# Third layer's q, k, v and gated input projections in three fp32r terms

## What is computed

```
hn = rms_norm_2(h, ln_mix[i])
z  = hn @ a_w_in[j]                       # 1024 x 3072
q, k, v, b_gate, c_gate, hc = split(z)    # six parts of 512
q, k = rope_partial(q), rope_partial(k)
attn = diff_attention(q, k, v, lam, lambda_init, a_subln[j])     # 4 heads, two maps each
conv = b_gate * causal_short_conv(c_gate * hc, a_conv_w[j])
h = h + concat([attn, conv]) @ a_w_out[j]
```

## Time and profile before

| | us |
|---|---|
| median of 3 runs | 1997.77 (1997.6 to 1998.2) |
| the profiled execution | 1994.57 |
| its span, first to last instruction | 1992.8 |
| PE busy in the span | 1924.8 (97%) |
| DVE busy | 1452.1 (73%) |
| ACT busy | 1013.4 (51%) |

### The profile page before, as it was taken

How to read it: one execution, slowest core, us unless ns; L and a number is a source line. 1 busy time by engine, 2 the same in 40 slices (tenths; PEclk the granted TensorE clock), 3 DMA queues, 4 the chain that set the end, 5 groups by cost and what they waited for, 6 DMA issues and landing times.

```text
span 1992.8 us, 30177 instructions
## 1 busy us (share of the span) xinstructions
PE 1924.8 (97%) x12687; PEld 1755.4 (88%) x12687; DVE 1452.1 (73%) x1742; ACT 1013.4 (51%) x1156; POOL 76.9 (4%) x122
## 2 busy tenths in 40 slices
PE   6999999999999999999999999999999999999997
PEld 5878878788788868999999898989898989898986
DVE  7888995774765346665455588888888888888873
ACT  3512121535465213444345577666676677667754
POOL 4010000000000100100220000000000000000000
PEclk9999999999999999999999999999999999999998
DMA  9945221453522431456753389999999999999981
GB/s 345 310 127 190 70 65 67 146 188 110 206 90 86 171 119 61 158 177 193 208 207 108 145 308 345 361 332 353 349 363 331 349 352 360 333 352 353 353 301 38
DMA packets 225858, 452.31 MB, mean 227 GB/s; under 512 B 6944, under 2 KB 91176, under 8 KB 225720
## 3 DMA queue, kind: packets, MB, share of 16 engines
q1 hardware_dynamic: 222128, 444.39, 63.6%
q0 software_dynamic: 1904, 5.80, 1.0%
q10 hardware_dynamic: 1688, 0.15, 0.1%
HBM read 448.21 MB, written 2.10 MB: 226 GB/s over the span
## 4 chain that ended last, share of the span: by engine, by line
PE 86%; DVE 8%; ACT 3%; issue 1%; DMA 1%; SPq 0%; POOL 0%; ACTq 0%; DVEq 0%; POOLq 0%
PE bank L1224 25%; PE bank L1250 12%; PE bank L2645 8%; PE bank L973 6%; PE bank L2411 4%; PE bank L1008 3%; PE bank L1056 2%; PE bank L856 2%; PE bank L897 2%; PE bank L774 2%; PE bank L1332 2%; PE bank L2906 1%; PE bank L762 1%; PE bank L2380 1%; PE bank L1235 1%
## 5 line engine op out<-in xcount | busy, mean ns | idle before, releaser
L2143 DVE TENSOR_TENSOR ring_r<-ring,his_r 128x2816 fp32r<-128x2816 f32 (+1 forms) x192 | 586.6, 3086 | 39.0 <-ACT his_r L1647 38.6
L1647 ACT ACTIVATE his_r<-ring 128x2816 fp32r<-128x2816 f32 (+1 forms) x192 | 491.0, 2561 | 185.7 <-DMA ring<-in_moe_w_dram 179.4
L1224 PE MATMUL bank<-his_r,hg_r 128*128 128x352 f32 x2048 | 353.4, 324 | 0.0
L1224 PEld LDWEIGHTS bank<-his_r,hg_r 128*128 128x128 f32 x2048 | 332.0, 188 | 0.6
L2645 PE MATMUL bank<-hT,ring 128*128 128x256 f32 x912 | 207.1, 383 | 1.4 <-ACT hT L3008 0.9
L2645 PEld LDWEIGHTS bank<-hT,ring 128*128 128x128 f32 x912 | 169.9, 190 | 27.9 <-issue 5.3
L1224 PE MATMUL bank<-ring_r,hg_r 128*128 128x352 f32 x1024 | 186.2, 324 | 0.0
L1224 PEld LDWEIGHTS bank<-ring_r,hg_r 128*128 128x128 f32 x1024 | 169.2, 189 | 0.0
L3293 DVE SCALAR_TENSOR_TENSOR arena<-ring,cw,arena 128x256 f32<-128x256 f32 x240 | 96.5, 477 | 0.1
L1250 PE MATMUL bank<-his_r,at_hi_r 128*128 128x512 f32 x352 | 92.9, 397 | 0.0
L1250 PE MATMUL bank<-his_r,at_lo_r 128*128 128x512 f32 x352 | 92.5, 396 | 0.0
(11 more groups left out here) (584 smaller groups left out, 3043.7 us busy)
## 6 DMA issues: line engine op xcount, KB each, us to landing
ring<-in_moe_w_dram SPq DMA_DIRECT2D x128, 1408.0 KB, 8.4
ring<-in_moe_w_dram SPq DMA_DIRECT2D x48, 1536.0 KB, 8.7
ring<-in_even_w_in_dram SPq DMA_DIRECT2D x28, 1024.0 KB, 6.2
ring<-in_ffn_w_dram SPq DMA_DIRECT2D x22, 1024.0 KB, 5.3
ring<-in_ada_w_dram SPq DMA_DIRECT2D x20, 1024.0 KB, 10.8
ring<-in_odd_w_in_dram SPq DMA_DIRECT2D x9, 2048.0 KB, 7.9
ring<-in_moe_w_dram SPq DMA_DIRECT2D x16, 1024.0 KB, 6.5
ring<-in_a_w_in_dram SPq DMA_DIRECT2D x6, 2048.0 KB, 7.9
```

The costliest lines, as they stand in the source:

```text
L1224: ins = mm(bank[first + m][:, 0:WC], x[:, KT // 2 * late + k, :], w[:, k, WC * m:WC * m + WC], start=(not late and k == 0 and s == "hg_hi" ...
L1647: A(moe_hi(n), moe_w(n), ACT.Copy).then_inc(sem("moe_hi"), 1)
L2143: V.tensor_tensor(moe_lo(n), moe_w(n), moe_hi(n).bitcast(F32), ALU.subtract).then_inc(sem("moe_lo"), 1)
```

## The change

It writes the input of `qk`, `v` and `bch` as a high part `hx_r` (in the place of `hT`) and a low part `xl_r` (in old gate space), cuts the weights into 12 halves of 128x2048 (u = 0 to 3 `qk`, 4 and 5 `v`, 6 to 11 `bch`), casts each half on ACT (`d_cast`) and subtracts on DVE (`d_low`), and multiplies three terms. The order of `qk` tiles 4 to 7 in PSUM changes to banks 7, 0, 1, 2.

```diff
+        with nc.sbuf_tensor("hx_r", [P, KT, T], F32R) as hx_r:    # over hT
+        xl_r = sb_r("xl_r", 7176, KT, T)
+        D_HI = [dw_r[off][:, :, :] for off in (19456, 11776, 21504, 25088, 27376, 19456, 11776, 25088, 27376, 25088, 27376, 25088)]
+        D_FREE = {5: ("qk", 2), 6: ("qk", 4), 7: ("qk", 8), 8: ("v", 2), 9: ("bch", 4), 10: ("bch", 6), 11: ("bch", 8)}
+        QK_BANK = (0, 1, 2, 3, 7, 0, 1, 2)
...
     TensorE
+            def d_tile(b, u, m):
+                hi, lo = D_HI[u], d_half(u, ring_r_flat)
+                pe.wait_ge(*d_hi(u))
+                for w, x in ((hi, 0), (lo, 0), (hi, 1)):
+                    if w is lo:
+                        pe.wait_ge(*d_lo(u))
+                    for k in range(KT):
+                        ins = mm(b[:, 0:T], w[:, k, m * P:m * P + P], x_low(k) if x else hx_r[:, k, :], ...)
+                ins.then_inc(acc_ready, 1)
+            def d_first():
+                pe.wait_ge(*took("oo", 6)); pe.wait_ge(*d_hi(0)); pe.wait_ge(*d_lo(0))
+                for k in range(KT):
+                    pe.wait_ge(*xg_waits(2)(k))
+                    for w in (hi, lo):
+                        for m in range(2):
+                            mm(bank[m][:, 0:T], w[:, k, m * P:m * P + P], hx_r[:, k, :], ...)
+                for k in range(KT):
+                    pe.wait_ge(*dx_lo(k))
+                    for m in range(2):
+                        ins = mm(bank[m][:, 0:T], hi[:, k, m * P:m * P + P], x_low(k), ...)
...
-            pe_gemm("qk", h, [], ready=xg_waits(2), lead=2, mid=norm_pair_rest, prev="oo", between=beside_qk)
-            pe_gemm("v", h, [took("qk", 6)], special={0: values2(0), 1: values2(1)}, between=beside_v)
+            d_first()
+            norm_pair_rest()
+            for q in range(2, KT):
+                if q < 4:
+                    pe.wait_ge(*took("oo", q + 5))
+                elif q >= 5:
+                    pe.wait_ge(*took("qk", q - 4))
+                d_tile(bank[QK_BANK[q]], q // 2, q % 2)
+                beside_qk(q)
+            for tt in range(TT):
+                pe.wait_ge(*took("qk", 6 + tt))
+                values2(tt)          # u = 4, 5: three terms of 8 matmuls of 256 columns each
+                beside_v(tt)
...
             def bch_tile(q):
+                d_tile(bank[6 + q % 2], 6 + q // 2, q % 2)
     ACT
+            def d_cast(u):
+                wait_chunk(act, name, v // 2, 0)
+                if u in D_FREE:
+                    act.wait_ge(acc_ready, phases[D_FREE[u][0]]["t0"] + D_FREE[u][1])
+                A(D_HI[u], d_half(u), ACT.Copy).then_inc(sem("q_hi"), 1)
             for q in range(KT):          # as oo tile q is taken
-                A(hT[:, q, :], xT[:, q, :], ACT.Identity, scale=gs[:, q:q + 1]).then_inc(sem("xg_ready"), 1)
+                A(hx_r[:, q, :], xT[:, q, :], ACT.Identity, scale=gs[:, q:q + 1]).then_inc(sem("xg_ready"), 1)
...
+                if q >= 5:
+                    d_cast(q - 5)
             root(2)
...
+            for u in range(3, 7):
+                d_cast(u)
             act.wait_ge(sem("pair_summed"), 2)
...
             take_gemm(act, "v", ...)
+            d_cast(7)
+            d_cast(8)
             act.wait_ge(sem("dve_made"), SET["lam"])
             A(small[:, 14:16], small[:, 14:16], ACT.Exp).then_inc(sem("lam_exps"), 1)
             def beside(b):
+                if b in (2, 4, 5):
+                    d_cast({2: 9, 4: 10, 5: 11}[b])
     DVE
+            def d_low(u):
+                dve.wait_ge(*d_hi(u))
+                V.tensor_tensor(d_half(u, ring_r_flat), d_half(u), D_HI[u].bitcast(F32), ALU.subtract)
+            def dx_low(k):
+                dve.wait_ge(sem("xg_ready"), k + 1)
+                V.scalar_tensor_tensor(x_low(k), xT[:, k, :], gs[:, k:k + 1], hx_r[:, k, :].bitcast(F32), ALU.mult, ALU.subtract)
+            # beside_oo: after the take of oo tile 6: d_low(0), dx_low(0) to dx_low(3)
+            # after the take of oo tile 7: dx_low(4) to dx_low(7), d_low(1), d_low(2), then the wait for the root
+            # beside_qk: d_low(3), d_low(4), d_low(5) at q = 3, 5, 6; d_low(6) and rotate(15) after q = 7
+            # d_low(7) after the sums for lambda
             def beside(b):
+                if b in (4, 5):
+                    d_low(6 + b)
                 if b < 8:
                     ...                   # the takes of the bch tiles of this b
+                if b in (0, 2):
+                    d_low(8 + b // 2)
```

More of the change, by code:

```diff
@@ L93, in build @@
             pass
+        with nc.sbuf_tensor("hx_r", [P, KT, T], F32R) as hx_r:
+            pass
         hT = sb("hT", [P, KT, T])
@@ L139, in build @@
         yb_r = sb_r("yb_r", 0, 2, KT, T)[:, :, :, :]
+        xl_r = sb_r("xl_r", 7176, KT, T)
+        dw_r = {off: sb_r(f"dw_r{off}", off, KT, T) for off in (19456, 11776, 21504, 25088, 27376)}
         cb_r = [sb_r(f"cb_r{n}", off, KT, T)[:, :, :] for n, off in enumerate((2048, 15360, 25088))]
@@ L549, in eo_done, with d_chunk, d_half, d_hi @@
             return phases[name]["t0"] + 2 * u + 2
+        D_HI = [dw_r[off][:, :, :] for off in (19456, 11776, 21504, 25088, 27376, 19456, 11776, 25088, 27376, 25088, 27376, 25088)]
+        D_FREE = {5: ("qk", 2), 6: ("qk", 4), 7: ("qk", 8), 8: ("v", 2), 9: ("bch", 4), 10: ("bch", 6), 11: ("bch", 8)}
+        QK_BANK = (0, 1, 2, 3, 7, 0, 1, 2)
+        def d_chunk(u):
+            return ("qk", u) if u < 4 else ("v", u - 4) if u < 6 else ("bch", u - 6)
+        def d_half(u, flat=ring_flat):
+            name, v = d_chunk(u)
+            return view(phases[name], v // 2, flat)[:, :, T * (v % 2):T * (v % 2) + T]
+        def d_hi(u):
+            return sem("q_hi"), 25 + u + 1
+        def d_lo(u):
+            return sem("q_lo"), 26 if u == 0 else 34 + u
+        def dx_lo(k):
+            return sem("q_lo"), 27 + k
+        def x_low(k):
+            return xl_r[:, (k + KT // 2) % KT, :]
         OO_HI = ["x0", "x1", "x2", "w0", "x3", "w1", "x4", "x5", "x6", "x7"] + [f"w{q}" for q in range(2, 8)]
@@ L859, in pe_rest @@
                 norm_pair(q)
-            def values2(tt):
[L862 to L866, removed]
+            def d_tile(b, u, m):
[5 more added lines that the diff above has]
+                    for k in range(KT):
+                        ins = mm(b[:, 0:T], w[:, k, m * P:m * P + P], x_low(k) if x else hx_r[:, k, :],
+                                 start=(w is hi and x == 0 and k == 0), stop=(x == 1 and k == KT - 1))
+                ins.then_inc(acc_ready, 1)
@@ new lines, in d_first @@
+            def d_first():
+                hi, lo = D_HI[0], d_half(0, ring_r_flat)
+                pe.wait_ge(*took("oo", 6))
+                pe.wait_ge(*d_hi(0))
+                pe.wait_ge(*d_lo(0))
+                for k in range(KT):
+                    pe.wait_ge(*xg_waits(2)(k))
+                    for w in (hi, lo):
+                        for m in range(2):
+                            mm(bank[m][:, 0:T], w[:, k, m * P:m * P + P], hx_r[:, k, :], start=(w is hi and k == 0), stop=False)
+                for k in range(KT):
+                    pe.wait_ge(*dx_lo(k))
+                    for m in range(2):
+                        ins = mm(bank[m][:, 0:T], hi[:, k, m * P:m * P + P], x_low(k), start=False, stop=(k == KT - 1))
+                        if k == KT - 1:
+                            ins.then_inc(acc_ready, 1)
@@ new lines, in values2 @@
+            def values2(tt):
+                for u in (4, 5):
+                    hi, lo = D_HI[u], d_half(u, ring_r_flat)
+                    pe.wait_ge(*d_hi(u))
+                    for w, x in ((hi, 0), (hi, 1), (lo, 0)):
+                        if w is lo:
+                            pe.wait_ge(*d_lo(u))
+                        for k in range(KT):
+                            ins = mm(bank[tt][:, T * (u - 4):T * (u - 4) + T], (x_low(k) if x else hx_r[:, k, :])[:, tt * P:(tt + 1) * P],
+                                     w[:, k, :], start=(w is hi and x == 0 and k == 0), stop=(w is lo and k == KT - 1))
+                ins.then_inc(acc_ready, 1)
@@ L892, in bch_tile @@
             def bch_tile(q):
-                w = wait_chunk(pe, "bch", q // 4, 0)
                 if q >= 2:
                     pe.wait_ge(*took("bch", q - 1))
-                for k in range(KT):
-                    ins = mm(bank[6 + q % 2][:, 0:T], w[:, k, (q % 4) * P:(q % 4 + 1) * P], h(k), start=(k == 0), stop=(k == KT - 1))
-                ins.then_inc(acc_ready, 1)
+                d_tile(bank[6 + q % 2], 6 + q // 2, q % 2)
             def logits2(b):
@@ L1905, in dve_rest, with beside_oo @@
             gated_lo(7)
-            take_gemm(dve, "oo", lambda q, lin, b: V.scalar_tensor_tensor(
-                xT[:, q, :], b, mod[:, 1, 16 + q:17 + q], xT[:, q, :], ALU.mult, ALU.add), between=lambda q: oo_low(q + 2) if q < 6 else None)
+            def d_low(u):
+                dve.wait_ge(*d_hi(u))
```

(30 more changed lines are left out.)

## The result

| | before | after |
|---|---|---|
| median, us (10 runs each) | 1997.99 | 2003.57 |
| lowest to highest | 1997.22 to 1999.88 | 2001.61 to 2004.95 |
| ratio of after to before, 95% interval | | 1.0026, 1.0016 to 1.0035 |
| span of the profiled execution | 1992.8 | 2000.2 |
| end of `oo` | 670.7 | 675.7 |

What follows compares the result with a forecast made beforehand. It took TensorE (PE) to bound the kernel, with DVE idle beside it; terms +1.8 + 1.9 - 5.8 + 3.8 + 0.8 + 0.6 gave +3.1 us, a median of 2000.9 us, range 1993.2 to 2006.0.

Steps and rivals of the forecast that it cites:

- PE's saving: qk, v and bch matmuls: three fp32r terms replace fp32, saving 14.0 us of PE if PE stays the bound everywhere.
- Step 1: Behind oo: long DVE subtractions hold POOL's norm additions, 3.8 us late; two tiles and the norm end 1.8 us later.
- the row of five pieces: Behind oo: five short DVE pieces of 0.5 us left a POOL addition at 0.79 us, so they were not charged.
- Step 2: Behind the norm-sum wait: PE's 4.4 us idle drops its clock, costing 1.9 us (bounds 0 and 2.9).
- Step 3: Six qk tiles and v: PE works without a stop and saves 5.8 us.
- step 4: Behind v: two ACT casts queued ahead of the Exp delay DVE's first scores and PE by 3.8 us.
- Step 5: Before the second logits: PE idles 6.3 us instead of 2.77, costing 0.8 us more clock loss (bounds 0 and 1.2).
- Step 6: Attention loop: PE and DVE wait for each other, 7.6 us eating the tiles' 7.0 us saving; +0.6 us net.
- the walk: Attention loop stepped through pass by pass in written order, giving 59.4 us from nlam to ao against 58.8 before.
- PE as the bound in the loop: Rival, attention loop: DVE's idle hides the subtractions, loop term -7.0, sum -4.5, 1993.3 us; chance 0.17.
- The held additions: Norm behind oo; the rival denied that POOL additions are held up: sum -2.6, 1995.2 us; chance 0.13.
- this rival: Attention loop: waits growing to about 2.8 us pull the clock down, about 4.6 us; +7.7, 2005.5 us; chance 0.20.

Runs made afterwards that it cites:

- kernel with three orders: Changed kernel with cast 7 before and cast 8 behind the Exp, loop casts and subtractions reordered, d_low(1) and d_low(2) moved off the POOL additions; 1985.52 us, ratio 0.9937.
- PE kept busy: Changed kernel plus 20 dummy fp32 matmuls before the norm-sum wait and 28 before the second logits; 1999.41 us, ratio 1.0004 to the kernel before.
- the Exp moved alone: Changed kernel with d_cast(7) ahead of the wait for the v sums and d_cast(8) behind the Exp; 1998.17 us, ratio 0.9999 to the kernel before.
- the next kernel: The kernel with three orders plus 12 dummy matmuls in TensorE's wait before the second logits; 1986.89 us, ratio 0.9945 to the kernel before.

## Why the prediction was right

It forecast 2000.9 us and +3.1; the change measured +5.6 and +2.0 in two comparisons, inside the range and on the side forecast. In the first pair of profiles the stretch grew by 3.5. That the sum came so close is in part luck: the clock cost more than forecast, the loop less.

- **PE's saving.** An fp32r tile is 2.84 us in the trace (5.67 for two), 2.87 in the sum. Right.
- **Step 1, +1.8.** Additions 3.8 us late: 4.0 in the profile, 1.8 to 1.9 per subtraction, shown by taking out one and both. The held ones were the fourth and fifth, not the third and fourth. PE's idle was 4.57, forecast 4.4. The rule of the Trainium skill ("GPSIMD Engine Reference", 8. Key points) that POOL contends with DVE instructions with two SBUF inputs agrees: the short pieces contend too. In the changed kernel it was mostly they that waited (2.90 against 1.67 us), and no addition was 0.1 us longer for it; in the kernel with three orders one was 0.57 longer. The forecast read the row of five pieces as 0.5 us each, but one of the five had taken 0.96 (the 961 ns of the earlier trace rows), which already showed a DVE piece that waits.
- **Step 2, +1.9.** With PE kept busy the first logits come 2.3 us earlier. Right in size, a little low.
- **Step 3, -5.8, and step 4, +3.8.** The first logits came at +46.7 (forecast 716.9 less 670.7, +46.2), `nlam` at +52.7 (+52.3). Moving the casts gave back 3.6.
- **Step 5, +0.8.** The fall behind the second idle cost 1.4 to 2.9 us. What I had not seen is that the kernel before does not always pay its own 1.7: it paid in the profile I had and not in the next. That is the mis-sized term; without that fall before, steps 2 and 5 together cost 3.8 to 5.2, not 2.7. It fits the larger +5.6. Where the clock fell in the timed runs is not recorded, only its mean in each: 0.985 to 0.989 in the first ten runs of the changed kernel (2003.57 us) and 0.987 to 0.991 in the second ten (2000.51). So the 3 us between the two sets go with the clock; how the 5.6 split into place and cause stays open.
- **Step 6, +0.6.** `nlam` to `ao`, steps 5 and 6 together: 60.2 forecast, 60.1 and 58.6 measured. At full clock, 57.1 with PE kept busy against 57.0 in the second profile of the kernel before, so the step itself cost 0.2, not 0.6. The waits before the transposes were 1.28, 0.81, 1.53 and 1.22 us and one of 0.71 before a tile, for my 1.6, 1.2, 1.9, 1.5 and 1.2: each 0.3 to 0.5 too long. My reading that DVE "has become as long as PE" was wrong as a cause: an order with the same work runs in 54.0 us. The step named the right waits and, for d_low(10), the right queue (DVE stood 1.72 us for cast 10, and 1.71 for cast 11, which the walk did not have), but called a matter of order one of amount.
- **Rivals.** PE as the bound in the loop did not happen as written, and happens in another order. The held additions are shown. The clock did not fall inside the loop: in both profiles of the changed kernel the windows behind 740 us read 1.00, with waits of up to 1.55 us. That waits below 2.77 are safe, as this rival took it, is not shown: in the kernel with three orders the clock fell behind waits of 1.27 and 0.40.

## What to carry to other kernels

When matmuls are made cheaper by work on other engines, price the work where it stands in each queue, not by the engine's idle share: here 13 us of gain and 2 to 6 of loss differ only in where four casts and six subtractions stand in their queues. Look first for a single short instruction that others wait for (an Exp, a row of additions) and put nothing long ahead of it, or beside it where the two engines hold each other up, as DVE and POOL did here. And measure a change of 0.2% by the stretch between two fixed points of the profile: it told 3.5 us where whole runs of one kernel differed by as much. Look behind its end too: a fall of the clock can slip out of the stretch, as the 1.6 us in `ao` did.

## What the runs showed that was not expected

- The same idle of 2.77 us pulled the clock down in one execution of the kernel before and not in the next, and that of 2.99 us did with the Exp moved alone and not with the three orders. Behind 2.63 us it held in the one profile that had it; behind 4.55 to 4.57 (five profiles) and 6.58 (six) it fell in every one. And it fell once behind waits of only 1.27 and 0.40 us, at the start of `ao` with the three orders (granted clock 0.83 from 770 to 780 us), where the same waits (1.25 and 0.40) left it at 1.00 in the next kernel.
- A DVE subtraction of 2.28 us held a POOL addition of 0.74 to 2.65 us and itself went to 2.8. Of the DVE pieces of 0.48 us, two went to 1.22 and 0.96 beside additions of 0.76 to 0.81, and two others, undisturbed, held an addition to 1.31.
- `oo`, whose matmuls are the same in both kernels, ended between 670.7 and 676.9 us in twelve profiles.
